# A two-layer diffusion step with routed experts: router by expert, last expert in whole, tokens turned first, and other orders of splits, sums, turns and copies

## The chip, the cores and the metric

The kernel runs on one core of a Trainium2 chip. The metric is device time in microseconds of one execution. A core has TensorE (PE; its weight loads are shown as PEld), VectorE (DVE), ScalarE (ACT), GpSimd (POOL) and SyncE (SP), which here only issues transfers. TensorE has two clock levels, 1.2 and 2.4 GHz; the profile shows the granted one as a share of the higher.

## The reference

Two sequences of 128 tokens with 1024 channels (a context prompt and noisy latents) go through two layers, then a final RMSNorm. In short:

```
for l in (0, 1):
    sh1, sc1, g1, sh2, sc2, g2 = split(silu(cond) @ w_ada[l] + b_ada[l])     # per sequence
    h = rmsnorm(x) * (1 + sc1) + sh1
    proj = h @ w_in[l]                    # low-rank q, kv latent, rotary key, pooling input u
    attn = softmax attention over own keys (latents also over 128 cached keys)
    x = x + g1 * (concat(attn, pooled(u) @ w_pool * pool_scale) @ w_out[l])
    h = rmsnorm(x) * (1 + sc2) + sh2
    layer 0:  y = (silu(h @ w_gate) * (h @ w_up)) @ w_down                   # 2816 wide
    layer 1:  logits = h @ w_router; top 2 of 8, softmax of the two
              y = sum over 8 experts of gate_e * swiglu_e(h)                 # 3584 wide each
    x = x + g2 * y
y = rmsnorm(x) * final_norm_g; also returned: the normalised kv latents and rotary keys
```

All data is float32.

## The kernel before, in words

Tokens of both sequences stand side by side as 256 columns. Up to the experts the activations lie turned (channels on partitions) in `xT`, eight blocks of 128 channels (`KD`). Weights come by SP through a ring of seven slots of 1 MB in the fixed order `STREAM`; an item is issued once the item that held its slot is used (`free`, L556 to L562). SP's queue runs the items strictly in that order.

**Splits.** The projections (`project`, L1480 to L1482) take each float32 product as three products of rounded halves. A weight item is two pieces; ScalarE makes the high half of a piece (`upto`, L698), VectorE the low half (L958), into rings of seven. The tokens are split into `hx` (ScalarE L736, VectorE L1022). Where an engine calls `upto` is written out by hand, and each engine runs its list in order.

**Norms.** `norm(t)`, t = 0 to 3, are the four norms ahead of the layers' halves. ScalarE squares pairs of blocks (`squares`, L714); for t > 0 VectorE adds the pairs onto the first (`add_squares`, L977), and TensorE sums over partitions with a column of ones (L1424: 8 records for two blocks, 32 for all eight at t = 0). ScalarE takes the root, VectorE the reciprocal, TensorE spreads it over partitions (`spread`, L1432), VectorE multiplies (L994), and VectorE and ScalarE apply shift and scale, four blocks each (L1014, L732).

**Modulation rows.** `mod_rows` (L1447) multiplies `silu_c` (128 by 32, two columns used) with a 1 MB item of `w_ada`; eight items make a group of rows. ScalarE copies the rows (`take_rows`, L743), TensorE turns them (`turn_mod`, L1457). These items are laid into places where TensorE waits anyway (`ADA_PLACES`).

**Start.** Small vectors and the two token tiles are loaded. TensorE waits for all small vectors and turns them (L1396), then turns the tokens (L1401); VectorE copies in the same order (L962, L966).

**Router and gather.** The logits are 16 products of tokens by the router's 8 columns (L1698; each product is two records). Then TensorE turns the normed tokens (L1705), VectorE finds the top two, the softmax weights and one-hots, TensorE counts ranks (L1711 to L1715), VectorE writes placing matrices `P` (L1232) and TensorE gathers the first expert's 96 places (`gather`, L1728) into banks 0 and 1. ScalarE copies the turned tokens (L850 to L853) and the first half of the gather (L858), VectorE the second (L1249).

**Experts.** Eight experts, each with eight gate/up steps of 512 columns and eight of 384 (`gate_up`, L1819) and fourteen down steps (`down`, L1834), weights through a ring of fourteen 1 MB slots, from L572 and L576. The result Y is split into high and low halves by ScalarE and VectorE (`take_Y` L872 to L876, `add_Y` L1267 to L1274), multiplied back to the tokens' places (`combine`, L1767), weighed (L1282) and added (L1289). For experts 0 to 6 this runs beside the next expert; for the last one nothing is beside it. A second to third round for an overfull expert stands under a test and does not run here.

**End.** Squares of the sums on ScalarE (L929), root (L934), reciprocal (L1366), one scaling of 1024 columns per sequence (L1368), one store per sequence (L628).

## Time and profile before

| what | value |
|---|---|
| median of 3 runs | 1400.64 us (1399.94 to 1402.57) |
| the profiled execution | 1400.27 us |
| its span | 1398.4 us |
| TensorE busy | 1347.7 us, 96% of the span |
| VectorE busy | 369.9 us, 26% |
| ScalarE busy | 249.0 us, 18% |
| read from memory | 463.33 MB, 332 GB/s over the span |
| gate and up products of the experts (L1819) | 582.1 us busy |
| down products (L1834) | 290.7 us busy |

The span is the time from the first to the last instruction of the profiled execution; its own device time is a little longer. "Busy" counts instructions in flight, so a busy TensorE may still run at half clock. The experts' stage runs from 484.6 to 1381.8 us of the span.

### The profile page before, as it was taken

What the parts mean: (1) busy time and instruction counts of PE and PEld (TensorE: products, weight loads), DVE (VectorE), ACT (ScalarE), POOL (GpSimd) and SP (SyncE); (2) the same over time, 40 slices, a digit from 0 to 9 for tenths busy, and PEclk for the clock granted to TensorE, in tenths of its full rate; (3) what the DMA queues carried; (4) which work ended last, traced back from release to release, by engine and by line L of the source; (5) the groups of instructions that cost most, each with busy time, mean ns of one, the idle gap of its engine ahead of it and who ended that gap; (6) DMA issues with size and microseconds to landing.
All of it is one profiled execution on the core that took longest, in us unless ns stands there. A gap on an engine that the chain in (4) does not pass through costs nothing.

```text
span 1398.4 us, 27658 instructions
## 1 busy us (share of the span) xinstructions
PE 1347.7 (96%) x12440; PEld 690.8 (49%) x12440; DVE 369.9 (26%) x591; ACT 249.0 (18%) x393; POOL 28.3 (2%) x60
## 2 busy tenths in 40 slices
PE   5999899999998999999999999999999999999995
PEld 3957699998857733333333333343333333333331
DVE  2425555555435501011111112011102111111213
ACT  2415544443423400000000000010000000000001
POOL 0030000000030000000000000000000000000000
PEclk9899999999999999999999999999999999999998
DMA  9787986563773899999999999999999999999970
GB/s 366 278 295 280 366 287 202 190 198 131 276 252 123 342 365 397 384 363 386 421 397 376 420 419 353 421 362 357 399 420 390 384 420 389 374 421 411 374 323 31
DMA packets 110793, 466.51 MB, mean 334 GB/s; under 512 B 9770, under 2 KB 52564, under 8 KB 73812
## 3 DMA queue, kind: packets, MB, share of 16 engines
q1 hardware_dynamic: 109696, 463.80, 85.1%
q8 instruction: 100, 1.64, 0.5%
q10 hardware_dynamic: 980, 0.94, 0.2%
q14 instruction: 17, 0.14, 0.0%
HBM read 463.33 MB, written 1.38 MB: 332 GB/s over the span
## 4 chain that ended last, share of the span: by engine, by line
PE 86%; DVE 3%; ACT 1%; issue 0%; ACTq 0%; DVEq 0%
PE ps L1819 41%; PE ps L1834 21%; PE ps L1480 4%; PE ps L1481 4%; PE ps L1482 4%; PE ps L1644 1%; PE ps L1643 1%; PE ps L1645 1%; PE ps L1767 1%; PE ps L1491 1%; PE ps L1747 1%; PE ps L1447 1%; DVE sq L994 1%; DVE sq L1014 0%; PE ps L1728 0%; PE ps L1566 0%
## 5 line engine op out<-in xcount | busy, mean ns | idle before, releaser
L1819 PE MATMUL ps<-ering,xg 128*32 128x512 f32 (+1 forms) x6144 | 582.1, 539 | 0.7 <-ACT xg L858 0.7
L1819 PEld LDWEIGHTS ps<-ering,xg 128*32 128x32 f32 x6144 | 198.9, 110 | 374.5 <-issue 373.7
L1834 PE MATMUL ps<-ering,eT 128*32 128x512 f32 x2688 | 290.7, 592 | 0.0
L1480 PE MATMUL ps<-hx,high 128*128 128x256 f32 x640 | 180.2, 282 | 12.8 <-DVE hx L1022 9.8
L1834 PEld LDWEIGHTS ps<-ering,eT 128*32 128x32 f32 x2688 | 87.0, 110 | 197.8 <-issue 197.8
L1481 PE MATMUL ps<-hx,high 128*128 128x256 f32 x640 | 179.3, 280 | 0.0
L1482 PE MATMUL ps<-hx,low 128*128 128x256 f32 x640 | 179.2, 280 | 0.0
L958 DVE TENSOR_TENSOR low<-ring,high 128x1024 fp32r<-128x1024 f32 x101 | 120.9, 1222 | 80.7 <-ACT high L698 80.6
L1480 PEld LDWEIGHTS ps<-hx,high 128*128 128x128 f32 x640 | 122.7, 192 | 16.0 <-issue 12.8
L1481 PEld LDWEIGHTS ps<-hx,high 128*128 128x128 f32 x640 | 122.8, 192 | 0.0
L1482 PEld LDWEIGHTS ps<-hx,low 128*128 128x128 f32 x640 | 122.5, 191 | 0.0
L899 ACT ACTIVATE sg<-ps 128x512 f32<-128x512 f32 (+1 forms) x48 | 26.1, 544 | 522.6 <-PE ps L1819 522.6
L698 ACT ACTIVATE high<-ring 128x1024 fp32r<-128x1024 f32 x101 | 103.7, 1056 | 68.4 <-PE ps L1482 37.2
L1331 DVE TENSOR_TENSOR sq<-sg,ps 128x512 f32<-128x512 f32 (+1 forms) x48 | 29.8, 621 | 302.5 <-PE ps L1819 300.6
L1267 DVE TENSOR_TENSOR Yl<-ps,Yh 96x512 fp32r<-96x512 f32 x8 | 5.5, 687 | 236.3 <-ACT Yh L872 236.3
L1282 DVE SCALAR_TENSOR_TENSOR sq<-ps,w_slot,xT 128x512 f32<-128x512 f32 x32 | 23.9, 747 | 149.1 <-PE ps L1767 149.1
L1447 PE MATMUL ps<-ring,silu_c 128*32 128x512 f32 x384 | 51.3, 663 | 0.0
L872 ACT ACTIVATE Yh<-ps 96x512 fp32r<-96x512 f32 x8 | 4.7, 592 | 246.9 <-PE ps L1834 246.9
L1643 PE MATMUL ps<-fx,high 128*128 128x256 f32 x160 | 44.3, 277 | 0.0
L1644 PE MATMUL ps<-fx,high 128*128 128x256 f32 x160 | 44.2, 276 | 0.0
L1645 PE MATMUL ps<-fx,low 128*128 128x256 f32 x160 | 44.2, 276 | 0.0
L1334 DVE STREAM_TRANSPOSE eT<-sq 128x512 f32<-128x512 f32 (+1 forms) x48 | 31.0, 646 | 1.7
(216 smaller groups left out, 731.3 us busy)
## 6 DMA issues: line engine op xcount, KB each, us to landing
ering<-in_moe_w_down SPq DMA_DIRECT2D x112, 1024.0 KB, 10.6
ering<-in_moe_w_gate SPq DMA_DIRECT2D x64, 1024.0 KB, 8.2
ering<-in_moe_w_up SPq DMA_DIRECT2D x64, 1024.0 KB, 10.4
ring<-in_w_ada SPq DMA_DIRECT2D x48, 1024.0 KB, 9.1
ering<-in_moe_w_gate SPq DMA_DIRECT2D x64, 768.0 KB, 6.0
ering<-in_moe_w_up SPq DMA_DIRECT2D x64, 768.0 KB, 7.5
ring<-in_ffn_w_gate SPq DMA_DIRECT2D x11, 1024.0 KB, 5.7
ring<-in_ffn_w_up SPq DMA_DIRECT2D x11, 1024.0 KB, 8.7
```

The source lines that it names most:

```text
L698: A(next(halves(q, raw)), raw, ACT.Copy).then_inc(high_ready, 1)
L958: V.tensor_tensor(lo, raw, hi, ALU.subtract).then_inc(low_ready, 1)
L1334: V.transpose(eT[s][:, g, :, :].rearrange("p (n o) t -> p n o t", o=2), hm[:, turn % 2, 0:width].rearrange("p (n r o) -> p n o r", r=32, o ...
L1447: last = mm(ps[32 * c:32 * c + 32, ROWS_BANK, :], silu_c[:, k, :], ring[:, n % SLOTS, c * ADA_CHUNK:(c + 1) * ADA_CHUNK], start=k == 0, st ...
L1480: mm(out, hi[:, k, :], xh, start=n == 0, stop=False)
L1481: mm(out, hi[:, k, :], xl, start=False, stop=False)
L1482: last = mm(out, lo[:, k, :], xh, start=False, stop=n == KD - 1)
L1643: mm(o, hi[:, 0, mc], xh, start=a, stop=False, skip_group_check=True)
L1644: mm(o, hi[:, 0, mc], xl, start=False, stop=False, skip_group_check=True)
L1645: last = mm(o, lo[:, 0, mc], xh, start=False, stop=z, skip_group_check=True)
L1819: last = mm(ps[32 * c:32 * c + 32, bank, 0:width].rearrange("p (n r) -> p n r", r=64), xg[:, kk, at, 32 * g:32 * g + 32], w[t][:, c, :, :] ...
L1834: last = mm(ps[32 * group:32 * group + 32, bank, :], eT[s][:, g, 2 * i + odd, :], w[:, odd, 512 * half:512 * (half + 1)], start=(s, i) == ...
```

## The change

Seven edits, numbered here for reading; the diff is cut to their core.

1. Start: the identity gets its own semaphore; TensorE turns the tokens first and the vectors after, and VectorE copies in that order. `x_ready` is raised by halves. At t = 0 VectorE adds the squares, and TensorE sums one pair.
2. Sums: which pairs TensorE sums is `((0,), (0, 3), (0, 1, 2, 3), (0, 3))[t]`; VectorE adds the rest, at t = 1 and 3 ahead of the wait for the last piece. At t = 2 it adds nothing.
3. `norm_b`: the high half of the first four blocks of tokens is made by VectorE instead of ScalarE.
4. VectorE's `upto` ahead of the pooled channels' low halves is taken out; the next `upto` does those pieces. In `mixer` two items of modulation rows move behind `turn_mod` and `spread`.
5. Router: its 8 columns are copied into `silu_c`; eight products of 32 router columns by 256 tokens, in four column groups, are copied out, turned and summed. All copies of gate rows go to ScalarE. The turned tokens are copied half by half, ahead of the softmax's exponential. The weights of the tokens are computed after the gather, from `oh[:, 0]`; ranks use `oh[:, 3]`.
6. The first gather goes to banks 6 and 7 and its first half is copied while the second is made; the first expert starts on the first half.
7. Last expert: Y is copied in whole and multiplied as float32 with the places as float32; ScalarE runs a `Sqrt` on one column ahead of its wait; scalings and stores are cut in halves of 512 columns.

```diff
+FIRST_BANK = 6
+SUMS = (0, 3, 5, 5, 7)
+        Y_whole, PT_whole = xg[:, 0:4, :, :].rearrange("p k e t -> p (k e t)")[:, 0:D], PT_now[:, :, :].bitcast(f32)
+        lgT = xg[:, 0:4, :, :].rearrange("p k e t -> p (k e t)")[:, 0:N2]
...
@@ sync: stores @@
             for b, to in enumerate((y_prompt, y_sample)):
-                sp.wait_ge(y_ready, b + 1)
-                sp.dma_start(to, yout[:, b, :]).then_inc(stored, 16)
+                for half in range(2):
+                    columns = slice(512 * half, 512 * (half + 1))
+                    sp.wait_ge(y_ready, 2 * b + half + 1)
+                    sp.dma_start(to[:, columns], yout[:, b, columns]).then_inc(stored, 16)
...
@@ scalar: norm_b, router, turned tokens @@
-                for q in range(2 if halves_too else 0):
-                    act.wait_ge((h_ready, h_last_ready)[q], t + 1)
-                    A(hx[:, 4 * q:4 * q + 4, 0, :], hT[:, 4 * q:4 * q + 4, :], ACT.Copy).then_inc(hxh_ready, 1)
+                if halves_too:
+                    act.wait_ge(h_last_ready, t + 1)
+                    A(hx[:, 4:8, 0, :], hT[:, 4:8, :], ACT.Copy).then_inc(hxh_ready, 1)
...
+                    act.wait_ge(router_in, 16)
+                    A(silu_c[:, :, 2:2 + NE], wr[:, :, :], ACT.Copy).then_inc(router_ready, 1)
...
+            for b in range(2):
+                for half in range(2):
+                    act.wait_ge(h2T_done, 2 * b + half + 1)
+                    A(h2[:, b, 512 * half:512 * (half + 1)], ps[:, 2 * b + half, :], ACT.Copy).then_inc(h2_ready, 1)
             act.wait_ge(top2_ready, 1)
             A(stat[:, 26:28], stat[:, 24:26], ACT.Exp).then_inc(e1_ready, 1)
...
@@ scalar: end @@
+            A(stat[:, 30:31], eps[:, 0:1], ACT.Sqrt)
             act.wait_ge(pieces_used, NE * E_ITEMS + MP0)
-            take_Y(1, Y_even_end, Y_end, Yh_end)
+            A(Yt[0:64, :], ps[0:64, 7, :], ACT.Copy).then_inc(Y_even_end, 1)
+            A(Y_whole[64:CAP, 512:1024], ps[96:128, 6, :], ACT.Copy).then_inc(Y_last_end, 1)
...
@@ vector: norm_b, mixer @@
                 if halves_too:
+                    dve.wait_ge(h_ready, t + 1)
+                    step(V.tensor_copy(hx[:, 0:4, 0, :], hT[:, 0:4, :]))
                     for q in range(2):
-                        dve.wait_ge(hxh_ready, 2 * t + q + 1)
+                        if q:
+                            dve.wait_ge(hxh_ready, t + 1)
...
-                upto(min(PIECE0[ITEM["ukv", l, 0]] + PIECES, within("ukv", l, 0)))
...
-                    dve.wait_ge(pieces_used, end("out", l, j))
                     if j > 1:
                         add_squares(2 * l + 1, (j - 1,))
+                    dve.wait_ge(pieces_used, end("out", l, j))
...
-                add_squares(2 * l + 1, (3,))
...
-            add_squares(2, (1, 2, 3))
...
@@ vector: logits, end @@
-            step(V.tensor_copy(lg, ps[:, 4, 0:16].rearrange("p (b e) -> p b e", b=2)))
+            V.tensor_copy(lgT, ps[:, 4, 0:N2]).then_inc(lgT_ready, 1)
+            dve.wait_ge(lg_turned, 1)
+            step(V.reduce_sum(lg, ps[:, 4, N2:2 * N2].rearrange("p (b c e) -> p b e c", b=2, c=4)[:, :, 2:2 + NE, :], AX.X))
...
-            add_Y(NE, 1, Y_even_end, Y_end, Yh_end, Yl_end, now_end)
+            V.tensor_copy(PT_now[0:CAP, :, :], PT[0:CAP, NE - 1, :, :]).then_inc(now_end, 1)
+            dve.wait_ge(pieces_used, NE * E_ITEMS + MP0)
+            V.tensor_copy(Y_whole[0:CAP, 0:512], ps[0:CAP, 6, :]).then_inc(Y_first_end, 1)
+            dve.wait_ge(Y_even_end, 1)
+            V.tensor_tensor(Y_whole[0:64, 512:1024], ps[64:128, 7, :], Yt[0:64, :], ALU.add).then_inc(Y_added_end, 1)
...
+            factor(0)
+            scaled(0, 0)
             mean(1)
-            scaled(1)
+            scaled(0, 1)
+            factor(1)
+            scaled(1, 0)
+            scaled(1, 1)
...
@@ tensor: norm, mixer, logits, first gather, end @@
-                blocks = 2 if t else KD
+                pairs = ((0,), (0, 3), (0, 1, 2, 3), (0, 3))[t]
...
                 norm(2 * l + 1)
-                mod_rows(gap[2:4])
                 turn_mod(3 * l + 2)
                 spread(2 * l + 1)
-                mod_rows(gap[4:])
+                mod_rows(gap[2:])
...
+            for k in range(KD):
+                c = 32 * (k % 4)
+                last = mm(ps[c:c + 32, 4, 0:N2], silu_c[:, k, :], hT[:, k, :], start=k < 4, stop=k >= 4)
+            last.then_inc(logits_done, 1)
+            pe.wait_ge(lgT_ready, 1)
             for b in range(2):
-                for k in range(KD):
-                    last = mm(ps[:, 4, b * NE:(b + 1) * NE], hT[:, k, b * T:(b + 1) * T], wr[:, k, :], start=k == 0, stop=k == KD - 1)
-            last.then_inc(logits_done, 1)
+                last = nc.tensor.transpose(ps[:, 4, N2 + b * T:N2 + (b + 1) * T], lgT[:, b * T:(b + 1) * T], ident)
+            last.then_inc(lg_turned, 1)
...
+                    if m == 3 and not rnd:
+                        last.then_inc(gat_half, 1)
...
-                    wait_xg(gathers_before(e, rnd))
+                    if begins and not rnd:
+                        pe.wait_ge(xg_first_ready, 1)
+                    else:
+                        wait_xg(gathers_before(e, rnd))
...
+            for b, half, bank in COMBINE_END:
+                if half:
+                    pe.wait_ge(Y_last_end, 1)
+                    pe.wait_ge(Y_added_end, 1)
+                else:
+                    pe.wait_ge(Y_first_end, 1)
+                mm(ps[:, bank, :], PT_whole[0:CAP, b, :], Y_whole[0:CAP, 512 * half:512 * (half + 1)], start=True, stop=True).then_inc(cmb_end, 1)
```

## Rows read from the trace of the kernel before

**Rows 1.** Windows: stretch, length, busy time (x instructions) of each engine, PEclk, DMA share, GB/s

```profile
160.00:170.00 10.00, 10.00 (x67) 10.00 (x67) 3.04 (x4) 4.08 (x5) 0.00 (x0) 0.75 1.02 351
...
470.00:500.00 30.00, 27.77 (x224) 17.64 (x224) 10.00 (x46) 6.96 (x11) 0.00 (x0) 0.89 1.00 409
500.00:530.00 30.00, 30.00 (x284) 10.16 (x284) 5.57 (x8) 2.98 (x5) 0.00 (x0) 1.00 0.91 343
```

**Rows 2.** Timeline of the start: start us, us, engine, line, operation, [idle before, releaser]

```profile
10.58 0.73 PE L1396 MATMUL ps<-cst,arena 128*128 128x128 f32 x2 [10.58 <-DMA arena<-in_kv_norm_g]
...
11.24 3.67 PE L1401 MATMUL ps<-cst,arena 128*128 128x128 f32 x16
...
14.85 1.92 PE L1447 MATMUL ps<-ring,silu_c 128*32 128x512 f32 x16
...
18.25 3.83 PE L1424 MATMUL ps<-ones,sq 128*128 128x1 f32 x32 [1.47 <-ACT sq L714]
...
29.71 0.60 ACT L743 ACTIVATE mrow<-ps 128x512 f32<-128x512 f32 x1 [7.34 <-PE ps L1447]
...
33.62 0.68 DVE L1004 CAST high<-ring 128x1024 fp32r<-128x1024 f32 x1
...
35.80 2.36 DVE L1022 TENSOR_TENSOR hx<-sq,hx 128x1024 fp32r<-128x1024 f32 x2 [0.23 <-ACT hx L736]
```

**Rows 3.** Tile views of transfers: second token tile, eighth ring item (landing us min/median/max)

```profile
L534 SPq DMA_DIRECT2D arena<-in_x_sample x1: 424/424/424, 1.7 to 1.7; - x1
...
DMA to landing us min/median/max: 4.0/4.5/5.0
...
L556 SPq DMA_DIRECT2D ring<-in_w_ada x1: 328/328/328, 16.0 to 16.0; - x1
...
DMA to landing us min/median/max: 9.9/10.3/10.7
```

**Rows 4.** Timeline, middle of layer 0

```profile
147.20 0.69 DVE L977 TENSOR_TENSOR sq<-sq 128x512 f32<-128x512 f32 x1 [0.75 <-DVE xT L1050]
...
148.93 1.92 PE L1447 MATMUL ps<-ring,silu_c 128*32 128x512 f32 x16
...
157.64 2.36 DVE L1022 TENSOR_TENSOR hx<-sq,hx 128x1024 fp32r<-128x1024 f32 x2 [1.12 <-ACT hx L736]
...
159.02 0.55 PE L1480 MATMUL ps<-hx,high 128*128 128x256 f32 x1 [3.56 <-DVE hx L1022]
```

**Rows 5.** Timeline, between the layers

```profile
345.83 2.28 DVE L977 TENSOR_TENSOR sq<-sq 128x512 f32<-128x512 f32 x3
```

**Rows 6.** Timeline, ahead of layer 1's output projection

```profile
431.07 3.48 DVE L958 TENSOR_TENSOR low<-ring,high 128x1024 fp32r<-128x1024 f32 x3
...
436.18 0.38 PE L1480 MATMUL ps<-hx,high 128*128 128x256 f32 x1 [2.95 <-DVE hx L1134]
```

**Rows 7.** Timeline, router, gather and first expert

```profile
468.70 3.81 PE L1698 MATMUL ps<-wr,sq 128*128 128x8 f32 x32 [1.02 <-DVE sq L1014]
472.36 3.54 PE L1705 MATMUL ps<-cst,sq 128*128 128x128 f32 x16
...
478.45 5.44 PE L1728 MATMUL ps<-P,h 128*128 128x96 f32 x32 [1.53 <-ACT h L853]
484.58 15.66 PE L1819 MATMUL ps<-ering,xg 128*32 128x512 f32 x144 [0.70 <-ACT xg L858]
```

**Rows 8.** Chain of waits at the end: start us, us, what

```profile
1369.75 12.06 PE ps L1834 x112
...
1385.35 0.76 DVE sq L1282
...
1390.37 1.28 ACT L934
...
1394.04 1.28 DVE h L1368
```

**Rows 9.** Timeline, float32 products of 512 columns in layer 1's attention

```profile
409.72 5.31 PE L1566 MATMUL ps<-ring,arena 128*128 128x512 f32 x12
```

More of the change, by code:

```diff
@@ L841, in _ @@
                 A(gate[:, b, 512 * half:512 * (half + 1)], ps[:, GATE_BANK[b, half], :], ACT.Copy).then_inc(gate_first_ready, 1)
+            for b, half in ((0, 1), (1, 0)):
+                A(gate[:, b, 512 * half:512 * (half + 1)], ps[:, GATE_BANK[b, half], :], ACT.Copy).then_inc(gate_last_ready, 1)
+            for b in range(2):
+                for half in range(2):
+                    act.wait_ge(h2T_done, 2 * b + half + 1)
+                    A(h2[:, b, 512 * half:512 * (half + 1)], ps[:, 2 * b + half, :], ACT.Copy).then_inc(h2_ready, 1)
             act.wait_ge(top2_ready, 1)
@@ L1367, in scaled @@
                 dve.wait_ge(yrs_ready, b + 1)
-                V.scalar_tensor_tensor(yout[:, b, :], xt[:, b, :], rt[:, b:b + 1], fin, ALU.mult, ALU.mult).then_inc(y_ready, 1)
+            def scaled(b, half):
+                columns = slice(512 * half, 512 * (half + 1))
+                V.scalar_tensor_tensor(yout[:, b, columns], xt[:, b, columns], rt[:, b:b + 1], fin[:, columns], ALU.mult, ALU.mult).then_inc(y_ready, 1)
             add_up(NE, 1, (0, 1, 2), cmb_end, gated_end, xt_end, COMBINE_END)
@@ L1392, in piece @@
                 return tuple(t[:, q % PIECES, :].rearrange("p (k n) -> p k n", k=k) for t in (high, low))
[L1394 to L1397 removed]
+            pe.wait_ge(ident_in, 16)
             pe.wait_ge(x_in, 32)
@@ L1402, in _ @@
             last.then_inc(xT_done, 1)
+            pe.wait_ge(small_in, 16 * 9)
+            for a, r in ((0, 128), (1, V_B_ROWS)):
+                last = nc.tensor.transpose(ps[:, 0, 128 * a:128 * a + r], vrow[0:r, a, :], ident[0:r, 0:r])
+            last.then_inc(vecT_done, 1)
             pe.wait_ge(ones_set, 1)
@@ L1417, in norm @@
                             last.then_inc(xt_done, 1)
-                if t:
-                    pe.wait_ge(sums_ready, 3 * t)
-                for k in range(blocks):
-                    if t == 0 and k % 2 == 0:
-                        pe.wait_ge(sq_ready, k // 2 + 1)
-                    for b in range(2):
-                        last = mm(ps[:, 0, b:b + 1], sq[:, k, b * T:(b + 1) * T], ones[:, 0:1], start=k == 0 and b == 0, stop=k == blocks - 1, skip_group_check=True)
+                for r in pairs:
+                    if r == 0 and t != 2:
+                        pe.wait_ge(sums_ready, SUMS[t + 1])
+                    else:
+                        pe.wait_ge(sq_ready, 4 * t + r + 1)
+                    for k in (2 * r, 2 * r + 1):
+                        for b in range(2):
+                            last = mm(ps[:, 0, b:b + 1], sq[:, k, b * T:(b + 1) * T], ones[:, 0:1], start=k == 0 and b == 0, stop=r == pairs[-1] and k % 2 == 1, skip_group_check=True)
                 last.then_inc(ss_done, 1)
@@ L1749, in gather_group, with combine @@
                 last.then_inc(gat_done, 1)
-            def combine(n, turns=range(4), now=now_ready, halves_of_Y=(Yh_ready, Yl_ready), combined=cmb_done, weighted=gated_ready, places=COMBINE):
+            def combine(n, turns=range(4)):
                 for r in turns:
-                    b, half, bank = places[r]
+                    b, half, bank = COMBINE[r]
                     if r == 0:
-                        pe.wait_ge(now, n)
-                    if places == COMBINE:
-                        if r == 2:
-                            pe.wait_ge(weighted, 4 * n - 2)
-                        for ready, parts in zip(halves_of_Y, (3, 2)):
-                            pe.wait_ge(ready, parts * n)
-                    else:
-                        for ready, parts in zip(halves_of_Y, ((1, 3), (1, 2))):
-                            pe.wait_ge(ready, parts[half])
+                        pe.wait_ge(now_ready, n)
+                    if r == 2:
+                        pe.wait_ge(gated_ready, 4 * n - 2)
+                    pe.wait_ge(Yh_ready, 3 * n)
+                    pe.wait_ge(Yl_ready, 2 * n)
                     for part, y in enumerate((Yh, Yl)):
                         last = mm(ps[:, bank, :], PT_now[0:CAP, b, :], y[0:CAP, 512 * half:512 * (half + 1)], start=part == 0, stop=part == 1)
-                    last.then_inc(combined, 1)
+                    last.then_inc(cmb_done, 1)
             def wait_xg(n):
@@ L1841, in expert @@
                             gate_up(s, kk)
+                            if begins and not rnd and s == 0 and kk == 2:
+                                wait_xg(1)
                             if s == 0 and kk in (2, 4):
```

132 lines of the change are left out of this document (66 added, 66 removed).

## The prediction

> **What bounds the kernel now.** I read the windows first, then the timeline around every place that the change touches, then the landings of transfers. In the expert stage TensorE is busy in every microsecond at full clock [rows 1], so whatever lets that stage begin earlier, and whatever shortens the end, moves the end. Ahead of it are the chains between two blocks of matmuls (a norm, its factors, the split of the tokens): there TensorE waits, and these are the places to price. The profiled execution took 1400.27 us, with a span of 1398.40 and 1.87 around it; the median of the runs shown, 1400.64, is 0.37 above it, and I add that at the end.
>
> **Start of the kernel.** Now TensorE begins at 10.58, when the last small vector has landed, turns vectors, then tokens for 3.67 [rows 2]. The second token tile was issued at 1.7 and landed 5.0 later, at 6.7 [rows 3]. New order: tokens 6.7 to 10.4, vectors to 11.3, the four 512-wide copies of tokens on VectorE (below 0.69 each) [rows 4] to 13.0, the vectors' copy, the conditioning's silu, and the first two items of modulation rows at about 13.8 where they ran at 14.85 [rows 2]. The sums of squares then cost TensorE 8 records instead of 32, 1.0 for 3.83 [rows 2], after three additions on VectorE (0.69 each) [rows 4], the last behind the last square, near 16.6. So the eight items could be through by 25 instead of 29.7 [rows 2]. But the eighth item was issued at 16.0 and landed at 26.7 [rows 3], behind seven that fill the queue from the start; issued earlier it would land no earlier. Its matmuls take 0.9 to 1.7 by clock, so the copy of the rows starts at 27.7 to 28.5 instead of 29.71: 1.2 to 2.0 won. Against it: the high half of the first four blocks is now rounded on VectorE, behind its first weight piece, where ScalarE did it beside; that adds about 0.5 (0.68 for a cast of this size, less the wait of 0.23) ahead of the subtraction [rows 2]. Sum: **-1.1** (0 to -2.0).
>
> **Middle of layer 0.** The chain is residual, square, addition, sums, root, factors spread. Two additions stood on it, the one before the residual and the one after the last square (0.69 each) [rows 4]. The first now runs before the wait for the last piece, the second is replaced by one more pair in the sums, 8 records, 0.95 (3.83 for 32) [rows 2]. That pair costs no more than the addition because TensorE does the first pair during the square. The root comes 0.5 earlier; then TensorE has two items of modulation rows fewer in front of the spread (1.92) [rows 4], which is 2.2 in all for the normed tokens. Six items stand behind the spread instead of four, 5.8 instead of 3.8 at 1.92 for two: begun near 149.6 they end near 155.3, before the tokens are split (156.4), so they cost nothing; if two or three of them ran at half clock they would end about 157 and take 0.6 back. The rounding on VectorE pays here: VectorE had stood idle 1.12 for ScalarE's copy before its subtraction [rows 4]; it now does its own copy in 0.7, 0.4 won. Sum: **-2.6** (-2.0 to -3.0).
>
> The matmuls behind it began at 159.02 after 3.56 of idle TensorE [rows 4] and ran on a granted clock of 0.75 over the ten microseconds from 160 [rows 1]: 5 of them at 1.2 GHz, and with 159.02 to 160 near 3.0 lost. The idle shrinks to about 1.3. Whether the clock then stays at 2.4 GHz the trace does not show; between 0 and -3.0 I take **-1.0**, nearer to nothing, because the sparse sums ahead are longer.
>
> **Between the layers.** The three additions (2.28) go, and TensorE waits only for the last square, which ends some 0.6 after the additions could begin at 345.83 [rows 5]; but it then does four pairs, 32 records, for 3.83 [rows 2]. Now: 8 records, 1.0, behind the additions' end at 348.1. New end 350.3 against 349.2, so 1.1 late; the spread and the rows after it ran at half clock there and may again. VectorE's own rounding gives 0.4 back, if the four items of rows behind the spread do not end last, in which case it is 1.5 in all. Sum: **+1.0** (+0.4 to +1.5). This edit alone costs.
>
> **Middle of layer 1, ahead of the output projection.** VectorE made three weight splits (3.48 from 431.07) in front of the low halves of the pooled channels, and TensorE waited 2.95 for those, to 436.18 [rows 6]. The splits go behind. What is late next: TensorE's own last turns, at 436.18 less 2.95, 433.2, and the heads' low halves, which follow ScalarE and are needed only by the second half of the first piece. Four pieces of 24 matmuls are split before that by an earlier call, so the moved splits are wanted only after all four. Sum: **-2.9** (-2.5 to -3.1).
>
> **Norm before the experts.** TensorE is busy without a gap from the projection through rows and token turns to the sums, so the additions taken away win nothing, and the extra pair adds 8 records: **+0.9** (0 to +1.0), by the same 3.83 for 32.
>
> **Router.** 32 records with 8 columns took 3.81 from 468.70 [rows 7]. By expert it is 16 records of 256 columns in four column groups: half of what 16 records of 512 take (1.92) [rows 4], so 1.0. New behind it: a copy out (about 0.4), two turns (0.4), and a sum over the groups in place of the copy (0.2): the logits stand at 470.9 instead of 472.7, -1.8. A low clock could double the first term. The token turns (16 records, 3.54, rows 7, at half clock; 1.8 at full) now run while VectorE picks experts; they end at 475.9, and the ranks stand behind them on TensorE, though the picking is ready by 474.5 (its dozen small operations take some 1.8 from the logits; 472.7 in the new order). Ranks then at 472.8 (full clock) or 474.2, one-hots 1.8 later, gather at 475.0 to 476.5 instead of 478.45. ScalarE now copies the turned tokens half by half, and its two table loads come after that: no longer before the gather. They may cost the first copy of the gather up to 0.5 if the gather is quick. VectorE's weights of tokens (some 1.3) move behind the low halves of the tokens, where the next thing wanted of it is fifteen microseconds away. The gather took 5.44 [rows 7]. The clock of 0.89 over thirty microseconds [rows 1] is 6.6 at half, shared by token turns and gather; with 3.4 of it here the gather is 3.7 at full. Its first half is copied while the second runs, so the wait of 0.70 goes [rows 7]. Experts begin 6.0 earlier with no low clock, 4.3 with one low stretch in the gather, 2.6 to 3.0 with two. I take **-4.8**, less than half of the way from one to none.
>
> **End.** After the last expert matmul, at 1369.75 and 12.06 later, the first weighing began at 1385.35 [rows 8], behind Y's high and low halves. With Y in whole: a copy (0.7), then one fp32 product. Twelve records of that width took 5.31 [rows 9], so a product of two is 0.9: first result at 1383.6, and each later one 0.9 apart, where weighing and adding take 1.4 for each. -1.75. If TensorE were at half clock the products would be 1.8 apart and this would shrink to about -0.5. The table load of 1.28 for the root [rows 8] moves under the last down projection: of it 1.1 is won, as the last square shares ScalarE. The two scalings of 1.28 are cut in halves; the last store carries 256 KB behind the last 0.68. In all VectorE ends at 1392.6 instead of 1395.3, and the store from there to the end of the span, 3.1 now, loses 0.4 (0 to 0.8). Sum: **-3.1** (-2.4 to -3.6).
> By the Trainium skill ("ScalarE: Activation LUTs", section on what ACT_TABLE_LOAD costs) a switch of tables takes 1283 ns and then a drain of about 1380 ns. The row shows the root only 0.01 behind the load, so here that drain is not seen; by the page the end would be -4.5.
> By the same skill ("DMA: Bandwidth & Descriptors", the two cost components) a transfer costs about 2.0 us and its bytes at 436 GB/s: half the bytes would save an estimated 0.6 of the 3.1.
>
> **Sum:** -1.1 - 2.6 - 1.0 + 1.0 - 2.9 + 0.9 - 4.8 - 3.1 = -13.6. From 1400.27: 1386.7, and with 0.37 **1387.0 us**. All low ends together give 1380, all high ends 1393.6; a round of independent terms stays within about 4.
>
> **Rivals.**
> (1) The weights cap the stage of the experts. For it: the transfer engines are busy 0.91 to 1.00 [rows 1], and TensorE takes three pairs of 1 MB items in 15.66 [rows 7], so it eats 400 GB/s, the rate of rows 1. Then an earlier start is given back and only the end is left: 1397.5. Against it: TensorE is busy 30.00 of 30.00, and the share is 0.91 just where the fourteen slots have filled, so the transfers catch up and wait for slots. 7%.
> (2) The low clock moves with the work: two low stretches over router and gather, one more at the start and on the projection of layer 1, 5 us back: 1392. For it: rows 1 show 0.89 in the thirty microseconds from 470 and the new order has more one-column sums and more short waits. Against: the router's own eight-column matmuls, after which it fell, are gone. 12%.
> The Trainium skill ("TensorE: Matmul & The Clock Gate", part 1) says that activity releases the throttle and idleness restores it, at a phase that is free of the kernel; it speaks for (2) at the longer waits.
> (3) Slower: TensorE enters the first expert at 1.2 GHz and stays. That costs half of each such microsecond; against a gain of 13.6 it decides from 27 us, and slower by 0.2% needs 33: 1403.6. For it only the weaker activity ahead; against it the clock is 1.00 from 500 on [rows 1], and the matmuls of an expert stand close. 2%.
> (4) The moved splits do nothing: ScalarE's halves or the heads are late as well and the projection starts where it did: 1389.9. Against: the idle of 2.95 is put down to the pooled low halves alone. 7%.
> The forecast with its own spread has 72%.
>
> **Chances.** A change under 0.2% (2.8 us) is what this measurement can't tell. Forecast, (2) and (4) are faster; so is (1), by 3.1, though only just, so half of it goes to the same: faster 0.95, same 0.03, slower 0.02. The range for 8 in 10 is 1383.0 to 1391.5: it takes in (4), most of (2), not (1).
>
> **What the profile after would show.** The first group of modulation rows copied at about 28; the first projection piece of the gate about 2.6 earlier relative to the sums before it; 32 records of sums between the layers, ending 1.1 later after the last down projection; no wait for VectorE ahead of layer 1's output projection; experts starting near 474 (484.58 less 10.5) and the stage itself still 897 long with no idle; 13.5 from the last expert matmul to the end of the span instead of 16.6. I am wrong if TensorE idles in the first expert, if the clock is low in it, or if the eighth item lands much before 26.

## The result and the profile after

In the first comparison the changed kernel took 1384.3 us (median of 4 runs, 1381.36 to 1387.22) and the kernel before 1401.6 us (4 runs, 1399.94 to 1408.44): a ratio of 0.9857, 95% interval 0.9835 to 0.9879. In a second comparison: 1387.48 against 1404.21, ratio 0.9879 (0.9857 to 0.9900). The median of these nine executions of the changed kernel is 1387.0, the forecast time, and that is luck: the forecast gain was too small (13.6 us, where the medians of the two comparisons are 17.3 and 16.7 apart and the intervals reach from 14 to 23), and the time that it was taken from was too low by nearly as much. The kernel before is slower than the runs that I started from: over the three comparisons that followed, 37 executions of it have a median of 1404.5 (1398.95 to 1411.75), and the one whose profile I priced from, 1400.27, lies near their fast end. The base of the forecast, 1400.64, is 3.9 below that median.

The profiled execution of the changed kernel took 1387.22 with a span of 1385.4, 13.0 less than the profiled one before. All readings of "after" below are from it.

Windows of the changed kernel (columns as in [rows 1]):

```profile
150.00:170.00 20.00, 18.73 (x161) 16.29 (x154) 14.82 (x20) 12.82 (x17) 0.00 (x0) 1.00 1.05 374
470.00:500.00 30.00, 30.00 (x266) 12.13 (x268) 5.96 (x20) 2.97 (x4) 0.00 (x0) 0.94 1.01 408
500.00:530.00 30.00, 30.00 (x320) 10.71 (x316) 4.88 (x7) 2.39 (x4) 0.00 (x0) 1.00 0.95 378
```

Against [rows 1] the granted clock at the gate projection is 1.00 instead of 0.75, and TensorE is busy in all of the thirty microseconds from 470 instead of 27.77.

Timeline of its start:

```profile
13.19 3.48 PE L1490 MATMUL ps<-ring,silu_c 128*32 128x512 f32 x16 [2.67 <-issue]
16.66 1.02 PE L1467 MATMUL ps<-ones,sq 128*128 128x1 f32 x8
...
26.82 1.93 PE L1490 MATMUL ps<-ring,silu_c 128*32 128x512 f32 x8 [1.48 <-DMA ring<-in_w_ada]
28.82 0.60 ACT L755 ACTIVATE mrow<-ps 128x512 f32<-128x512 f32 x1 [10.84 <-PE ps L1490]
...
35.05 0.69 DVE L1043 CAST hx<-sq 128x1024 fp32r<-128x1024 f32 x1
35.77 2.36 DVE L1048 TENSOR_TENSOR hx<-sq,hx 128x1024 fp32r<-128x1024 f32 x2
```

As priced, the rows start earlier (13.19 against 14.85), the sums are 8 records, and the eighth item still waits for its transfer, at 26.82. Then its products run at half clock, 1.93 where the same eight records take 1.06 at 152.31 (below), and the subtraction starts at 35.77 where it started at 35.80 [rows 2].

Middle of layer 0, and between the layers:

```profile
144.93 1.28 ACT L734 ACT_TABLE_LOAD   x1
...
146.22 0.26 ACT L734 ACTIVATE rt<-ps,eps 128x2 f32<-128x2 f32 x1
...
147.45 4.50 PE L1490 MATMUL ps<-ring,silu_c 128*32 128x512 f32 x40
...
152.31 1.06 PE L1490 MATMUL ps<-ring,silu_c 128*32 128x512 f32 x8 [0.36 <-DMA ring<-in_w_ada]
152.91 2.36 DVE L1048 TENSOR_TENSOR hx<-sq,hx 128x1024 fp32r<-128x1024 f32 x2
...
154.29 0.36 PE L1523 MATMUL ps<-hx,high 128*128 128x256 f32 x1 [0.92 <-DVE hx L1048]
...
338.98 3.73 PE L1467 MATMUL ps<-ones,sq 128*128 128x1 f32 x32
...
350.75 0.35 PE L1523 MATMUL ps<-hx,high 128*128 128x256 f32 x1 [0.95 <-DVE hx L1048]
```

The six items of rows (48 records) end at 153.4, before the projection can start, and the idle ahead of it is 0.92 instead of 3.56 [rows 4].

Ahead of layer 1's output projection, the router and the gather:

```profile
428.28 0.27 PE L1656 MATMUL ps<-cst,arena 64*128 64x64 f32 x1
428.48 0.38 PE L1523 MATMUL ps<-hx,high 128*128 128x256 f32 x1
...
461.99 1.07 PE L1741 MATMUL ps<-sq,silu_c 128*32 128x256 f32 x16 [1.02 <-DVE sq L1037]
463.60 0.44 PE L1745 MATMUL ps<-cst,xg 128*128 128x128 f32 x2 [0.55 <-DVE xg L1210]
463.88 1.91 PE L1752 MATMUL ps<-cst,sq 128*128 128x128 f32 x16
...
468.57 5.41 PE L1777 MATMUL ps<-P,h 128*128 128x96 f32 x32 [1.05 <-DVE P L1258]
473.91 15.66 PE L1866 MATMUL ps<-ering,xg 128*32 128x512 f32 x144
```

Nothing waits ahead of 428.48 any more (2.95 in [rows 6]). From the router's first record to the experts it is 11.92 instead of 15.88 [rows 7], and the first expert follows the gather without idle.

Chain of waits at the end (start us, us, what):

```profile
1367.65 3.48 PE ps L1881 x32
1371.13 0.02 issue
1371.15 0.70 DVE xg L1386
1371.85 0.87 issue
1372.72 1.11 PE ps L1946 x2
1373.83 0.02 issue
1373.86 0.76 DVE sq L1308
...
1381.48 0.75 DVE h L1405
1382.23 0.66 DVEq L296
```

No table load is left on it [rows 8]. After the copy of Y, TensorE takes 0.87 more to begin: that is the part which I had not priced.

### The profile page after: what moved, and what is told of

It is laid out like the page before. It is cut to its first block, busy times and chain, and to the rows that moved or that the text cites. A ratio compares the mean times of both kernels' runs of the same rounds, so it can differ in the third digit from the quotient of the medians.

```text
span 1385.4 us, 27659 instructions
## 1 busy us (share of the span) xinstructions
PE 1345.8 (97%) x12442; PEld 684.9 (49%) x12442; DVE 368.9 (27%) x591; ACT 247.1 (18%) x392; POOL 28.3 (2%) x60
## 4 chain that ended last, share of the span: by engine, by line
PE 94%; DVE 3%; DMA 2%; issue 1%; ACT 0%; SPq 0%; DVEq 0%
PE ps L1866 42%; PE ps L1881 21%; PE ps L1523 5%; PE ps L1524 5%; PE ps L1525 5%; PE ps L1534 2%; PE ps L1490 2%; PE ps L1685 1%; PE ps L1687 1%; PE ps L1686 1%; PE ps L1814 1%; DMA ring<-in_w_ada 1%; PE ps L1798 1%; PE ps L1609 1%; DVE sq L1037 1%
## 5 line engine op out<-in xcount | busy, mean ns | idle before, releaser
L1523 PEld LDWEIGHTS ps<-hx,high 128*128 128x128 f32 x640 | 121.5, 190 | 11.1 <-issue 10.9
L1524 PEld LDWEIGHTS ps<-hx,high 128*128 128x128 f32 x640 | 121.1, 189 | 0.0
```

The lines of the kernel that those rows point to most:

```text
L1523: mm(out, hi[:, k, :], xh, start=n == 0, stop=False)
L1524: mm(out, hi[:, k, :], xl, start=False, stop=False)
```

## The experiments

All comparisons are with the kernel before on the same chip. The first four kernels below were measured in one comparison, the next four in a second on the same chip, the last four in a third on another chip. "Low clock" and "half clock" are 1.2 GHz, and a low stretch is an unbroken time at it. My theory after the first comparison was that each step does what it was priced at and the rest of the gain is low clock that the kernel before has more of than its one profile shows. The rival was that a step gives more by itself than I had priced, which undoing it alone would show.

**The changed kernel again.** 

> The changed kernel once more, unaltered. Its profiled execution was 13.1 us under the profiled one of before, the medians 17.3 apart. Theory 1 (the steps are worth about 13 to 14 us; the rest is where low-clock stretches and a slower pace of the projections happened to fall in single executions): another profile of it is 2 to 6 us shorter with the experts starting 2 to 6 earlier, the difference lying in low-clock stretches ahead of the experts and in the projections' pace (0.114 or 0.118 us a product); and the paired difference is 14 to 20. Theory 2 (a step was worth more than I gave it): the difference between two profiles of this same kernel is under 1 us, and the first one was not typical only by its total.

Measured: 1387.48 (1383.29 to 1388.77), ratio 0.9879 (0.9857 to 0.9900). The profile was not what my first theory said: its span is 1385.7, 0.3 longer than the first one's and not 2 to 6 shorter, and its experts start at 474.38. Two profiles of this kernel that agree within 1 us are what the second theory said. So if single executions mislead, it is that of the kernel before, which two more profiles of it were taken for. It has 10 us more of low clock ahead of the experts than the first, and yet they start only 0.5 later.

**The end alone.** The kernel before, with the last expert's part of the change only:

```diff
-            take_Y(1, Y_even_end, Y_end, Yh_end)
+            A(Yt[0:64, :], ps[0:64, 7, :], ACT.Copy).then_inc(Y_even_end, 1)
+            A(Y_whole[64:CAP, 512:1024], ps[96:128, 6, :], ACT.Copy).then_inc(Y_last_end, 1)
...
+                mm(ps[:, bank, :], PT_whole[0:CAP, b, :], Y_whole[0:CAP, 512 * half:512 * (half + 1)], start=True, stop=True).then_inc(cmb_end, 1)
```

> The kernel before with the change's end alone (last Y in whole, Sqrt ahead of the wait, halves in the scalings and stores). Theory 1: from the last expert matmul to the end of the span 14.3 us instead of 16.6, so 2.3 less in time (2.0 to 2.6), and nothing else moves. Rival (my forecast's term): 3.1 less. In it TensorE starts the first whole product 0.8 to 0.9 after VectorE's copy has ended.

Measured: 1400.93 (12 runs), ratio 0.998 (0.9966 to 0.9993), so 2.8 us less (1.0 to 4.8). In its profile it is 14.13 from the last expert matmul to the end of the span, where the three profiles of the kernel before have 16.63, 16.63 and 16.64: 2.5 less, not 3.1. Timeline of its first product:

```profile
1381.23 0.69 DVE L1366 COPY xg<-ps 96x512 f32<-96x512 f32 x1 [28.95 <-PE ps L1855]
...
1382.62 3.67 PE L1914 MATMUL ps<-xg,PT_now 96*128 96x512 f32 x8 [1.45 <-DVE xg L1366]
```

The copy ends at 1381.92; the product begins 0.70 later.

**The start as before.** The changed kernel, with vectors turned first (not in this cut of the edit) and all four pairs of squares summed by TensorE at the first norm:

```diff
-                pairs = ((0,), (0, 3), (0, 1, 2, 3), (0, 3))[t]
+                pairs = ((0, 1, 2, 3), (0, 3), (0, 1, 2, 3), (0, 3))[t]
```

> The changed kernel with the old start: vectors turned before tokens, and all eight blocks of squares summed by TensorE at t = 0. Theory 1 (the eighth modulation item bounds the start, and what is won there goes to the low clock and to the rounding moved to VectorE): first projection piece 0 to 1.5 later than in the changed kernel, time +0 to +1.5. Rival (the new start is worth its whole 1.6 to 2 ahead of the norm's factors): +1.6 to +2.5.

Measured: 1390.03 (1386.91 to 1390.98), ratio 0.990 (0.9882 to 0.9919), 2.6 above the changed kernel. Its first projection (timeline) begins 1.1 later than the 36.93 of the changed kernel's second profile and 0.9 later than the 37.14 of its first:

```profile
38.05 0.55 PE L1522 MATMUL ps<-hx,high 128*128 128x256 f32 x1 [6.23 <-DVE hx L1048]
```

The start is later as my theory had it; the time went up by more than its 1.5, to the rival's side, by a difference that the intervals do not tell from either. Six profiles with the new start have their first projection at 35.60 to 37.14, mean 36.4, and five with the old one at 37.17 to 38.86, mean 38.1: the start is worth 1.7 by these means.

**The splits back.** The changed kernel, with the three weight splits again ahead of the pooled channels:

```diff
+                upto(min(PIECE0[ITEM["ukv", l, 0]] + PIECES, within("ukv", l, 0)))
```

> The changed kernel with VectorE's weight splits put back ahead of the pooled channels' low halves. Theory 1 (they alone held layer 1's output projection): TensorE waits about 3 for VectorE there again, time +2.7 to +3.2. Rival (the heads or ScalarE are nearly as late): under +1.5.

Measured: 1392.15 (1388.38 to 1392.95), ratio 0.991 (0.989 to 0.9929), 4.7 above the changed kernel. Timeline:

```profile
425.11 3.48 DVE L981 TENSOR_TENSOR low<-ring,high 128x1024 fp32r<-128x1024 f32 x3
...
430.23 0.38 PE L1524 MATMUL ps<-hx,high 128*128 128x256 f32 x1 [2.95 <-DVE hx L1161]
```

The three splits and the wait of 2.95 of [rows 6] are back to the hundredth, so rival (4) is wrong. What the time has beyond 3.0 is within the interval; its profile also took 13.51 from the logits to the experts, against 11.92, with 6.8 us at half clock there.

**The kernel before, a second profile.** 

> The kernel before, unaltered, for a second profile of it. Its executions went from 1399.6 to 1411.8 on this chip with a median of 1404.2, and the profiled one of 1400.27 is near their lower end. Theory 1 (my terms hold; the profile I counted from was a fast execution of before, so the size was short by what a typical one loses to the clock and the pace of products): this profile is 1 to 6 us longer, with the experts starting later by it and the whole difference in low-clock stretches and pace ahead of them. Theory 2 (a step of the change is worth more than its term): this profile agrees with the first within 1 us.

Measured: 1405.2, span 1403.3. A window of the first profile of this kernel that [rows 1] does not have, then windows of the second:

```profile
150.00:170.00 20.00, 16.44 (x118) 12.87 (x111) 10.26 (x17) 10.72 (x16) 0.00 (x0) 0.83 1.02 371
```

```profile
150.00:170.00 20.00, 16.44 (x133) 12.20 (x133) 10.51 (x18) 11.44 (x19) 0.00 (x0) 0.91 1.02 376
470.00:500.00 30.00, 27.16 (x194) 20.23 (x197) 12.73 (x54) 9.68 (x17) 0.00 (x0) 0.77 0.97 395
```

The same program is 4.9 longer in the span. The clock of 0.77 over thirty microseconds is 13.8 of them at 1.2 GHz, where the first profile has 6.6 [rows 1]; its gather took 6.08 instead of 5.44.

**The router as before.** The changed kernel, with the logits by token again:

```diff
-                last = mm(ps[c:c + 32, 4, 0:N2], silu_c[:, k, :], hT[:, k, :], start=k < 4, stop=k >= 4)
...
+                    last = mm(ps[:, 4, b * NE:(b + 1) * NE], hT[:, k, b * T:(b + 1) * T], wr[:, k, :], start=k == 0, stop=k == KD - 1)
```

> The changed kernel with the old logits: 16 products of tokens by 8 router columns, straight from the bank. Theory 1 (by the rows: 3.8 of logits and 0.2 of copy against 2.35 from the first product to the reduced logits): gather 1.7 to 1.9 later after the logits' start, and one low stretch more, +1.7 to +3.5. Rival (the token turns behind the logits hide most of it, as they did before): under +1.0.

Measured: 1391.67 (1389.2 to 1393.58), ratio 0.9916 (0.9894 to 0.9939), against 0.9879 (on the same chip) and 0.9857 for the changed kernel: 5 to 8 us of its gain by the ratios, with intervals that reach down to 1, and 3.7 by the stage in the profiles. A window of it, then its timeline:

```profile
470.00:500.00 30.00, 29.62 (x248) 13.88 (x252) 7.77 (x30) 3.91 (x6) 0.00 (x0) 0.90 0.93 360
```

```profile
470.38 6.53 PE L1771 MATMUL ps<-P,h 128*128 128x96 f32 x32 [1.05 <-DVE P L1256]
476.84 14.37 PE L1860 MATMUL ps<-ering,xg 128*32 128x512 f32 x132
```

From the logits to the experts it is 15.67, against 11.92 and 11.94 in two profiles of the changed kernel. The logits themselves explain 1.8 of that; the gather of 6.53, at half clock for most of its time, and token turns of 2.55 against 1.91, the rest. One profile doesn't settle that, because the stage varies: over the nine profiles with the new form it takes 10.31 to 13.51, mean 11.9, with 0 to 6.8 us at half clock in it, mean 3.4. The five with the old form take 15.67 to 18.10 and have 6.8 to 13.7 us, mean 9.6. So with the old form there was more low clock behind the logits, and with the new one the stage gains more than the 1.8 of its instructions. That the form of the logits is what brings the clock down is argued from one edit and these counts; it is not shown.

**Squares added by VectorE.** The changed kernel, with one pair in TensorE's sums at the second and third norm too:

```diff
-                pairs = ((0,), (0, 3), (0, 1, 2, 3), (0, 3))[t]
+                pairs = ((0,), (0, 3), (0,), (0,))[t]
```

> The changed kernel with the squares between the layers and ahead of the experts added by VectorE again, TensorE summing one pair. Theory 1 (my terms, +1.0 and +0.9 of the change): -1.5 to -2.0, of it 0.6 to 1.1 between the layers (sums to first projection) and 0.9 ahead of the experts. Rival (the three additions are as late as the 32 records): between the layers 0, in all -0.9.

Measured: 1386.69 (1382.52 to 1387.54), ratio 0.9869 (0.9844 to 0.9894): not told apart from the changed kernel. The profile has both terms of the expectation: 195.53 from the gate projection to layer 1's first, against 196.46 in the changed kernel's first profile, with the same 3.4 us of low clock in it, so 0.9 less; and 8 records of sums in 0.95 ahead of the experts, against 16 in 1.84. But it took 15.06 from the last expert matmul to the end, where that one took 14.34, because low clock fell on the end's products.

**The three improvements together.** As above, and ScalarE makes the first high half, and TensorE reads the flag for further rounds ahead of the last expert:

```diff
+                    if t == 0:
+                        act.wait_ge(h_ready, 1)
+                        A(hx[:, 0:4, 0, :], hT[:, 0:4, :], ACT.Copy).then_inc(hxh_ready, 1)
...
+                    pe.wait_ge(over_ready, 1)
+                    seen.append(pe.value_load(over[0:1, 0:1]))
...
-            pe.wait_ge(over_ready, 1)
-            more = pe.value_load(over[0:1, 0:1])
+            more = seen[0]
```

> sums_vector with two more edits: at t = 0 ScalarE makes the high half of the first four blocks again, and TensorE reads the overflow flag ahead of the last expert instead of after it. Theory 1: against the changed kernel -1.5 to -2.0 from the sums, 0 to -0.5 at the start, and at the end -0.8, since the first whole product then starts 0.1 and not 0.88 after VectorE's copy: -2.8 in all, 14.3 from last down product to the end becomes 13.5. Rival for the 0.88 (it is a wait for a later copy or the start-up of the product, not the flag and branch): the end stays 14.3 and the total is about -2.

Measured: 1384.03 (1379.84 to 1387.97), ratio 0.9851 (0.9826 to 0.9877). The copy of Y in it ends at 1372.96 and the product begins at 1373.48 (timeline), 0.52 later instead of 0.87 and 0.71:

```profile
1372.27 0.69 DVE L1393 COPY xg<-ps 96x512 f32<-96x512 f32 x1 [28.79 <-PE ps L1888]
...
1373.48 3.67 PE L1955 MATMUL ps<-xg,PT_now 96*128 96x512 f32 x8 [1.28 <-DVE xg L1393]
```

The end takes 13.98, not the 13.5 that I expected, so most of the delay is something else. Even the flag's part is not shown: over the nine profiles that read it late the delay is 0.59 to 1.10 (mean 0.8), over the two that read it early 0.52 and 0.63, and two of the nine have 0.6 as well. The whole may be 1 to 3 us faster than the changed kernel; the intervals overlap, and I don't call it faster.

**Keeping TensorE busy ahead of the first projection.**

```diff
+                    if l == 0 and i == 0:
+                        for x in range(12):
+                            mm(ps[:, 5, 0:128], ones[:, :], ident, start=True, stop=True)
```

> The changed kernel with twelve more float32 products of 128 columns on TensorE in the idle before layer 0's first projection piece; nothing reads them. Theory A (the times of both kernels follow how long TensorE runs at 1.2 GHz, and the longer waits bring that about): the idle of the changed kernel before the projection is filled, the projection begins where it did (within 0.3 us) and its first ten microseconds, at 1.2 GHz in both profiles of the changed kernel, run at 2.4 GHz; 1 to 2.5 us less, some 1385.5 beside 1387.5 in the earlier comparison, and a mean clock of 0.990 or more. Theory B (the clock's low stretches come at their own times, whatever the work): the low stretch stays or comes a few microseconds later, and the time is that of the changed kernel within 1 us. If the projection begins over 1 us later, the products were too many and neither is tested.

Measured: 1386.23 (1383.91 to 1391.35), ratio 0.9865 (0.9843 to 0.9886). In the version above, the same products:

> The same twelve products in the version with VectorE adding squares, ScalarE rounding the first high half and TensorE reading the overflow flag before the last expert. That version alone: 1384.0 in the earlier comparison. Theory A: 1382 to 1383. Theory B: 1384.

Measured: 1385.2 (1381.76 to 1387.51), ratio 0.9849 (0.9831 to 0.9867), where that version had 0.9851. Timeline and window of the first:

```profile
29.83 2.40 PE L1560 MATMUL ps<-cst,ones 128*128 128x128 f32 x20
35.78 0.55 PE L1523 MATMUL ps<-hx,high 128*128 128x256 f32 x1 [3.55 <-DVE hx L1048]
```

```profile
34.00:44.00 10.00, 8.22 (x48) 8.25 (x48) 9.96 (x11) 7.07 (x8) 0.00 (x0) 0.66 1.10 359
```

And of the second:

```profile
29.67 4.19 PE L1567 MATMUL ps<-cst,ones 128*128 128x128 f32 x24
35.39 0.35 PE L1530 MATMUL ps<-hx,high 128*128 128x256 f32 x1 [1.53 <-DVE hx L1052]
```

```profile
34.00:44.00 10.00, 8.61 (x73) 8.64 (x74) 9.98 (x11) 7.91 (x8) 0.00 (x0) 1.00 1.10 359
```

In one the products left 3.55 of idle and the projection ran on 0.66; in the other 1.53, and it ran on 1.00. That is what theory A says, but in two single profiles, and neither time improved. The test filled too little of the idle to decide.

The second profile also shows what low clock can do to the new end (timeline):

```profile
1368.42 1.52 PE L1958 MATMUL ps<-xg,PT_now 96*128 96x512 f32 x3 [1.39 <-DVE xg L1393]
...
1371.90 4.43 PE L1958 MATMUL ps<-xg,PT_now 96*128 96x512 f32 x5 [1.95 <-issue]
```

The products of Y stop for 1.95, which nothing in the profile explains, and go on at half clock; the end takes 16.51, as long as before the change.

**Two items of rows back ahead of the spread.**

```diff
+                mod_rows(gap[2:4])
...
-                mod_rows(gap[2:])
+                mod_rows(gap[4:])
```

> The changed kernel with two items of modulation rows moved back ahead of the spread in the middle of layer 0. If the step that I priced (these two items delay the spread by their 1.92 us) is right, the gate projection begins 1.5 to 1.9 later behind the sums than in the changed kernel and the time is 1.5 to 1.9 longer. Rival: the spread is held up by VectorE's small operations anyway, and then nothing changes. Theory A on the clock adds: the idle ahead of the gate projection is longer by as much, so a low stretch there returns, 1 to 3 us more.

Measured: 1389.78 (1388.53 to 1392.35, 4 runs), ratio 0.9894 (0.9877 to 0.9911): 2.1 more of 1404 than the second comparison of the changed kernel, 5.2 more than the first, and the intervals overlap with both. Timeline and window:

```profile
155.43 0.35 PE L1523 MATMUL ps<-hx,high 128*128 128x256 f32 x1 [2.85 <-DVE hx L1048]
```

```profile
150.00:170.00 20.00, 17.00 (x138) 14.92 (x131) 14.22 (x19) 13.71 (x19) 0.00 (x0) 0.91 1.06 379
```

From the sums to the gate projection it is 11.61 instead of 10.11: the moved items are worth 1.5. And with the longer idle the low clock is back at the gate projection: 0.91 over twenty microseconds, 3.6 of them at 1.2 GHz, where the changed kernel has 1.00. This doesn't hang on one profile. In all fourteen, those with 2.85 to 3.56 of idle ahead of the gate projection (this one, the three of the kernel before and the end alone) have 0.76 to 0.91 in 150 to 170; the nine with at most 1.5 of idle have 1.00, but for one with 0.98. Two of the nine (the changed kernel's second profile and the first with products added) have 3.4 us of low clock earlier, at 146 to 151: there it fell on rows that had time to spare, and sums to gate projection took 10.25 and 10.40 instead of 10.11.

**The kernel before, a third profile.** 

> The kernel before, unaltered, for a third profile. If one execution of it differs from the next by its low clock stretches, the span lies between 1398 and 1404, and its difference from the two other profiles is the difference in the time that these three spent at 1.2 GHz ahead of the experts, halved, within 1.5 us.

Measured: 1405.01, span 1403.2. Windows:

```profile
150.00:170.00 20.00, 16.44 (x111) 11.15 (x104) 9.50 (x16) 8.96 (x15) 0.00 (x0) 0.76 0.95 342
470.00:500.00 30.00, 27.15 (x207) 20.07 (x209) 14.20 (x57) 11.17 (x21) 0.00 (x0) 0.83 1.00 410
```

Ahead of the experts the three profiles of this kernel have 34, 41 and 48 us at 1.2 GHz, summed over half-microsecond windows from 11 to 489, in spans of 1398.4, 1403.3 and 1403.2. Halved differences of 3.4 and 6.8 stand against 4.9 and 4.8: the first meets my bound of 1.5 just so, the second misses it with 2.0. Between the second and the third profile I had 3.4 to expect and the spans differ by 0.1, which misses it clearly. So the amount of low clock doesn't give the span to better than some 3 us: it also depends on whether TensorE has work then, and on the pace of the projections (last section). The stage of the experts is 897.2 in all.

## Why the prediction fell short

The spans split at the first record of each stage. "Pair" is after less before in the two first profiles; "mean" is the same over all profiles whose kernel has the old or the new form of that stage (4 or 5 old, 3 for the end; 6 to 10 new). The row from the gate leaves out the kernel with two items of rows put back, whose low clock there comes from its idle; with it the mean is -1.3. The pair sums to 13.0, the means to 14.2.

| stage | predicted | pair | mean |
|---|---|---|---|
| to the first projection | -1.1 | 0.0 | -1.7 |
| layer 0, projections and attention | 0 | -2.3 | -0.2 |
| from the output projection to the gate projection | -2.6 | -2.4 | -3.2 |
| gate to layer 1's first projection (clock and sums) | 0.0 | -2.7 | -1.7 |
| layer 1, projections and attention | 0 | +2.7 | +1.1 |
| ahead of the output projection | -2.9 | -3.0 | -3.0 |
| output projection and norm ahead of the router | +0.9 | +1.0 | +1.3 |
| router and gather | -4.8 | -4.0 | -4.5 |
| experts | 0 | 0.0 | 0.0 |
| end | -3.1 | -2.3 | -2.3 |

**What held.** The splits, to a tenth. The middle of layer 0, though its 1.9 for two items of rows was 1.5 in its own experiment. The additional sums: +1.0 and +0.9 were forecast, and both were 0.9 when undone. The norm ahead of the router. Experts at 473.91 (forecast 474) with a stage of 897.2, so rival (1) fell; from 470 on the clock recovers before the first expert, so rival (3) fell as well.

**The step that failed** is the clock, in two places of the prediction: the term at the gate projection, -1.0 "nearer to nothing", and the base, one execution with 0.37 added. At the gate projection the profile before has 6.0 us at half clock, to 165, and the one after none: -3.0. The other +0.3 of the -2.7 is the 0.9 that the sums cost, less what the low stretch between the layers gave back (6.8 us before, 3.4 after). Of the three profiles before, all have low clock in 150 to 170 (0.83, 0.91, 0.76); after the change it is 1.00 in both profiles, and it falls again below 0.98 only in the kernel whose idle was put back. So of the 3.0 that the prediction had priced there, this pair gave all, and it had taken a third. At the router the three before have 6.6 to 13.8 us at half clock in thirty, and the changed kernel 3.6. I had priced these places from the execution that had least of it at the router. Over 37 executions of the kernel before, the mean granted clock runs from 0.974 to 0.985 and the time falls by 9 us for each 0.01 of it; the median is 0.980, and my profile's 0.984. The nine of the changed kernel have 0.984 to 0.991, median 0.987. By that slope 6 us of the gain between the medians are clock. The forecast had 1.0 of it at the gate and 1.8 at the router (-4.8, where two low stretches, as before, gave -3.0), so 3 too little, which is what the gain is short by. The profiles agree: ahead of the experts the four with the old forms have 40 us of low clock on average, the ten made from the changed kernel 30, and half of that is 5 us. A slope over executions is no experiment, though, so this sum is argued and not shown. What remains open: the means over stages give 14.2, the profiled executions 16 (three of before, two of after) and the medians 17; I have no trace of the timed executions and can't place the last 2 or 3. The 14.2 is also near to 13.6 partly by luck, since terms that were too small (the start, the middle of layer 0, the gate) and too large (the router, the end, layer 1 at nothing) cancel.

**The start** was priced at -1.1 and showed nothing in the pair, because the profiled execution before began its first projection at 37.17, and four other profiles with the old start at 38.05 to 38.86. Put back by itself the old start costs 0.9 to 1.1 against the changed kernel's two profiles, and 1.7 by the means over all. The mechanism was right, and the pair of profiles alone would have said that it failed.

**Rival (2)** is half right: low stretches did move. Layer 1's latent projections ran at half clock at 381.5 to 385 after the change (1.7 of the +2.7 in "pair"; the other 1.0 is the pace of the projections, last section), and the start has 17 us of it against 10 to 14. But in sum there is less: 27 and 38 us against 34 to 48, summed as above. The Trainium skill ("TensorE: Matmul & The Clock Gate", part 1) says that the penalty of the ramp is under 1% of a typical span. For the start alone the three profiles of the kernel before agree: 10 to 14 us of low clock up to 44, halved 5 to 7 us, at most 0.5%. But with the low stretches that come later, up to the experts, it is 17 to 24 us, 1.2 to 1.7%, so the start alone is too little to reckon with here.

**The end** gave 2.3 of 3.1. The first weighing began 2.73 after the last expert matmul (1373.86 less 1371.13), against 3.54 before [rows 8]; I had it at 1.8. I had let TensorE start when VectorE's copy ended, and it starts 0.5 to 1.1 later in the eleven profiles with this end: this is the mis-sized term, and what makes up the delay is open. A risk that I had named and not weighed came true in four of the eleven: low clock on the four products, which take 5.4 instead of 3.67 in three of them. The end is then 14.41 to 15.06, and 16.51 in the fourth; in the other seven it is 13.98 to 14.34. In the three profiles of the kernel before, the clock fell only behind the last product. The table load did come off the chain, and the last transfer is 0.5 shorter: 2.5 from VectorE's end at 1382.89 to the end of the span, against 3.1 in [rows 8]. By the Trainium skill ("DMA: Bandwidth & Descriptors", the two cost components) half the bytes save an estimated 0.6, and this trace agrees to a tenth. The Trainium skill ("ScalarE: Activation LUTs", what ACT_TABLE_LOAD costs) also counts a drain of about 1380 ns to each load; the load at 144.93 ends at 146.21 and the root starts at 146.22, so this trace does not show it.

## What to carry to other kernels

Where a kernel has many short waits of TensorE, take two or three profiles of the kernel before, and price a change from the mean of each stage, not from one execution: here one profile was 4.9 us off the other two, and a part that works looked as if it did nothing. Price a wait that goes, or a run of narrow matmuls, with the clock behind it as well as with its own length. And where a product waits for another engine's copy, as at the end here, don't start it in the sum when the copy ends: here 0.5 to 1.1 us lay between.

## What the hardware showed that I had not expected

At full clock a stretch of projection matmuls runs at one of two paces. Groups of lines over layer 1's first projection, the changed kernel and then the kernel before (columns: shapes, count, busy us, mean ns):

```profile
L1525 PE MATMUL ps<-hx,low 128*128 128x256 f32 x69 | 19.4, 281 | 0.0
```

```profile
L1482 PE MATMUL ps<-hx,low 128*128 128x256 f32 x72 | 19.9, 276 | 0.0
```

The stage took 28.34 and 27.31 us. It isn't the change: the kernel before's third profile has 281 ns and 28.34 as well, and four kernels made from the changed one (the start as before, two items of rows back, both with products added) have the faster pace. What sets it is open.
